# Expert weights w1 and w3 in chunks of 1024 columns in place of 512, in a two-layer encoder with eight experts

## The reference: what is computed

```python
def swiglu(x, w1, w3, w2):
    return (jax.nn.silu(x @ w1) * (x @ w3)) @ w2

def moe_swiglu(h, router_w, w1, w3, w2):
    logits = (xf @ router_w).astype(jnp.float32)
    top_val, top_idx = lax.top_k(logits, TOP_K)
    gates = jax.nn.softmax(top_val, axis=-1)
    ...
    y = lax.map(expert_block, (buf_tok.reshape(n_blocks, EXPERT_BLOCK), block_exp))
    y = y.reshape(P, D) * buf_g[:, None].astype(y.dtype)
```

## Time and profile before

| | us |
|---|---|
| time, three runs | 1866.17, 1866.32, 1866.81 |
| median | 1866.32 |
| span of the profiled execution, first to last instruction | 1863.3 |
| PE busy with matmuls | 1699.1 (91%) |
| DVE busy | 1319.9 (71%) |
| ACT busy | 1015.6 (55%) |
| POOL busy | 58.0 (3%) |
| share of DMA queue 1, 473 MB | 70.2% of 16 engines' span |

### The profile page before, as it was taken

The page is one execution under the profiler, slowest core; times in us unless marked ns, Lnnn a source line. Parts: engine busy times, 40 slices in busy tenths (PEclk is TensorE's granted clock), DMA queues, the critical chain, the costliest instruction groups (busy, mean ns, idle before and its releaser), DMA issues.

```text
span 1863.3 us, 23242 instructions
## 1 busy us (share of the span) xinstructions
PE 1699.1 (91%) x8214; PEld 1387.5 (74%) x8215; DVE 1319.9 (71%) x1525; ACT 1015.6 (55%) x1259; POOL 58.0 (3%) x52
## 2 busy tenths in 40 slices
PE   2996799999998999799999997997997997997998
PEld 2854699997677787588887785786786786786786
DVE  6597388885333799355554996896896896896897
ACT  1215344442322787344443875885775785775775
POOL 0000000000000100000000100100100100100100
PEclk7997899999998999899999998998998998999999
DMA  9972357867622499355553997897897898798790
GB/s 344 359 271 91 99 215 282 318 247 272 225 91 90 180 365 369 112 193 186 181 181 137 327 373 251 318 372 260 298 373 280 288 372 291 271 367 312 262 370 25
DMA packets 206838, 475.89 MB, mean 255 GB/s; under 512 B 6429, under 2 KB 8618, under 8 KB 206650
## 3 DMA queue, kind: packets, MB, share of 16 engines
q1 hardware_dynamic: 206442, 473.45, 70.2%
q10 hardware_dynamic: 208, 0.07, 0.0%
HBM read 472.46 MB, written 1.05 MB: 254 GB/s over the span
## 4 chain that ended last, share of the span: by engine, by line
PE 86%; DVE 6%; issue 5%; ACT 2%; DMA 1%; SPq 0%; DVEq 0%; ACTq 0%
PE bank L894 18%; PE bank L896 18%; PE bank L895 18%; PE bank L555 9%; PE bank L836 3%; PE bank L659 2%; PE bank L660 2%; PE bank L661 2%; PE bank L548 2%; PE bank L846 2%; PE bank L903 1%; DVE ada_acc L1257 1%; DVE w_lo L1562 1%; PE bank L679 1%; PE bank L677 1%
## 5 line engine op out<-in xcount | busy, mean ns | idle before, releaser
L1562 DVE TENSOR_TENSOR w_lo<-ring,w_hi 128x1024 fp32r<-128x1024 f32 x672 | 830.1, 1245 | 271.1 <-ACT w_hi L1156 199.7
L1156 ACT ACTIVATE w_hi<-ring 128x1024 fp32r<-128x1024 f32 x672 | 713.2, 1061 | 302.1 <-PE bank L896 288.8
L894 PE MATMUL bank<-w_hi,hg_hi 128*128 128x512 f32 x1008 | 398.9, 396 | 4.7 <-DVE w_lo L1562 4.3
L896 PE MATMUL bank<-w_hi,hg_lo 128*128 128x512 f32 x1008 | 394.8, 392 | 0.0
L895 PE MATMUL bank<-w_lo,hg_hi 128*128 128x512 f32 x1008 | 394.3, 391 | 0.0
L894 PEld LDWEIGHTS bank<-w_hi,hg_hi 128*128 128x128 f32 x1008 | 189.0, 188 | 69.0 <-issue 9.7
L896 PEld LDWEIGHTS bank<-w_hi,hg_lo 128*128 128x128 f32 x1008 | 189.3, 188 | 41.5
L895 PEld LDWEIGHTS bank<-w_lo,hg_hi 128*128 128x128 f32 x1008 | 189.5, 188 | 30.4
L894 PE MATMUL bank<-w_hi,hid_hi 128*128 128x512 f32 x504 | 202.2, 401 | 0.1
L896 PE MATMUL bank<-w_hi,hid_lo 128*128 128x512 f32 x504 | 197.7, 392 | 0.0
L895 PE MATMUL bank<-w_lo,hid_hi 128*128 128x512 f32 x504 | 197.1, 391 | 0.0
(11 more groups left out here) (260 smaller groups left out, 1837.5 us busy)
## 6 DMA issues: line engine op xcount, KB each, us to landing
ring<-in_moe_w SPq DMA_DIRECT2D x168, 2048.0 KB, 8.2
ring<-in_ada_w SPq DMA_DIRECT2D x24, 2048.0 KB, 11.5
ring<-in_ffn_w SPq DMA_DIRECT2D x15, 2048.0 KB, 12.7
ring<-in_da_w_in SPq DMA_DIRECT2D x6, 2048.0 KB, 19.8
ring<-in_gla_w_in SPq DMA_DIRECT2D x6, 2048.0 KB, 11.3
ring<-in_da_w_out SPq DMA_DIRECT2D x2, 2048.0 KB, 11.1
ring<-in_gla_w_out SPq DMA_DIRECT2D x2, 2048.0 KB, 8.6
ring<-in_ffn_w SPq DMA_DIRECT2D x3, 1024.0 KB, 5.9
```

Source lines behind the costliest of these rows:

```text
L894: mm(out[:, :], xhi, whi[:, cs], start=first, stop=False)
L896: last = mm(out[:, :], xlo, whi[:, cs], start=False, stop=end)
L1156: A(w_hi[:, q % PIECES, :], raw_piece(q), ACT.Copy).then_inc(hi_done, 1)
L1562: v.tensor_tensor(w_lo[:, q % PIECES, :], raw_piece(q), w_hi[:, q % PIECES, :].bitcast(F32), ALU.subtract).then_inc(lo_done, 1)
```

## The change

Chunks of w1 and w3 have 1024 columns, the last one 512 (`ECW`), so an expert has four chunks in place of seven. A slot of a wide chunk is one half of the rows (four tiles of 128) with 1024 columns, so its rows are 4 KB as those of w2; a wide chunk takes two slots of w1, then two of w3, then the two of w2 of the chunk before. The number of slots, pieces, matmuls and bytes stays.

With one block of tokens, pieces are used in the order in which they lie. Each of the two halves of a w1 piece goes to a bank of its own (0 and 1), and of a w3 piece too (6 and 7). Silu, product, `hid_hi` and `hid_lo` come in pairs, on four occasions and not seven; a pair has the work of two of the old ones. The transposes, eight of them together, go to banks 4 and 5, and w3 of the next chunk waits for the product (`s_ea`) and no more for `hid_lo`. The product is written over silu and no more to `ada_acc`.

With two blocks, all eight banks are taken, and the halves of 512 columns are worked through as before (`halves_of_expert`): both w1 slots and both w3 slots of a wide chunk are read for the first 512 columns and again for the second.

SP waits for `slot_left`, which PE raises at the end of the first matmul of a slot's last piece, in place of `lo_done`. With two blocks a slot is only counted when all slots before it in the order have been left too (`hfreed`).

At an expert's start ACT and DVE split one piece, handle the gathered tokens, and then split two more. The four scattered banks are copied before pieces 2, 3, 4 and 5. The wait for `s_gl` on PE stands ahead of the branch.

```diff
+ECW = [1024, 1024, 1024, 512]
+ECH = len(ECW)
+EHALF = EF // FW
...
     for c in range(ECH):
-        order += [("w1", c), ("w3", c)]
+        order += [(what, c, part) for what in ("w1", "w3") for part in range(parts_of(c))]
         if c:
-            order += [("w2", c - 1)]
-    return order + [("w2", ECH - 1)]
+            order += [("w2", c - 1, part) for part in range(parts_of(c - 1))]
+    return order + [("w2", ECH - 1, part) for part in range(parts_of(ECH - 1))]
+
+def halves_of_expert(eorder):
+    slot_of = {key: i for i, key in enumerate(eorder)}
+    pieces = []
+    for s in range(EHALF):
+        c, h = divmod(s, 2)
+        for what in ("w1", "w3"):
+            if parts_of(c) == 2:
+                pieces += [(what, s, slot_of[what, c, part], kp, h, 4 * part + 2 * kp)
+                           for part in range(2) for kp in range(2)]
+            else:
+                pieces += [(what, s, slot_of[what, c, 0], p, None, 2 * p) for p in range(PPC)]
+        if s:
+            c, h = divmod(s - 1, 2)
+            pieces += [("w2", s - 1, slot_of["w2", c, h], p, None, p) for p in range(PPC)]
...
+    left_at = {}
+    for q, piece in enumerate(hpieces):
+        left_at[piece[2]] = q
+    hfreed, latest = {}, -1
+    for i in range(PER):
+        latest = max(latest, left_at[i])
+        hfreed[latest] = hfreed.get(latest, 0) + 1
...
-                    sp.wait_ge(lo_done, (e + back) * EQ + FQ + (j + 1) * PPC)
+                    sp.wait_ge(slot_left, (e + back) * PER + j + 1)
...
+            def expert_block(e):
...
+                            k, o = (4 * part + p, j) if parts_of(c) == 2 else (2 * p + j, 0)
+                            xhi, xlo = hg_hi[:, k, 0:P], hg_lo[:, k, 0:P]
+                            out = psum[(0 if what == "w1" else 6) + o]
...
+                        begun = mm(out[:, :], xhi, whi[:, cs], start=first, stop=False)
+                        if j == 0 and p == PPC - 1:
+                            begun.then_inc(slot_left, 1)
...
+            def expert_two_blocks(e):
...
+                            if b == 0 and j == 0 and q in hfreed:
+                                begun.then_inc(slot_left, hfreed[q])
...
-                    if q in (2, 5, 8, 11):
-                        copy_scattered(e, (q - 2) // 3)
+                    if q in (2, 3, 4, 5):
+                        copy_scattered(e, q - 2)
...
+                        for b in range(parts_of(c)):
+                            last = A(silu_e[:, b, :], psum[b][:, :], ACT.Silu)
...
+                        for b in range(parts_of(c)):
+                            last = v.tensor_tensor(silu_e[:, b, :], silu_e[:, b, :], psum[6 + b][:, :], ALU.mult)
```

More of the change, by code:

```diff
@@ L1176, in expert @@
-                    if what == "w3" and p == 0:
+                    what, c, part = eorder[i]
+                    if what == "w3" and q == PPC * first_slot["w3", c]:
                         act.wait_ge(w_free, e * EQ + FQ + PIECES + q)
                         if c:
-                            act.wait_ge(s_ea, e * ECH + c)
-                        for b in range(nb):
+                            act.wait_ge(s_et, e * EHALF + c)
+                        for b in range(parts_of(c)):
+                            last = A(silu_e[:, b, :], psum[b][:, :], ACT.Silu)
+                        last.then_inc(s_esl, EHALF - ECH + 1 if c == ECH - 1 else 1)
@@ new lines, in expert_block, with expert_two_blocks, split_up_to @@
+                    if q - 1 in turn_at:
+                        turn = turn_at[q - 1]
+                        act.wait_ge(s_et, e * EHALF + turn + 1)
+                        for b in range(parts_of(turn)):
+                            last = A(hid_1[0][:, turn % 2, b * 512:(b + 1) * 512], psum[4 + b][:, :], ACT.Copy)
+                        last.then_inc(s_hdh, EHALF - ECH + 1 if turn == ECH - 1 else 1)
+            def expert_two_blocks(e):
+                done = [0]
+                seen = set()
+                def split_up_to(q_end):
+                    while done[0] <= min(q_end, EQ - 1):
+                        q = done[0]
+                        if hpieces[q][2] not in seen:
+                            seen.add(hpieces[q][2])
+                            wait_landed(act, PRE + hpieces[q][2], e)
+                        act.wait_ge(w_free, e * EQ + FQ + q + 1)
+                        A(split_half(w_hi, q), raw_half_piece(q), ACT.Copy).then_inc(hi_done, 1)
+                        done[0] += 1
+                split_up_to(0)
+                gathered(e, 2 * P)
+                split_up_to(AHEAD)
+                gates_out(e, 2)
+                for q, (what, s, i, p, h, k0) in enumerate(hpieces):
+                    if q in (2, 3, 4, 5):
+                        copy_scattered(e, q - 2)
+                    split_up_to(q + AHEAD)
+                    if what == "w3" and q == hfirst["w3", s]:
+                        act.wait_ge(w_free, e * EQ + FQ + PIECES + q)
+                        if s:
+                            act.wait_ge(s_et, e * EHALF + s)
+                        for b in range(2):
@@ L1194, in _ @@
                 nb = act.value_load(nbk[0:1, bass.ds(e, 1)], min_val=1, max_val=2)
-                for n in (1, 2):
-                    with act.If(nb == n):
-                        expert(e, n)
+                with act.If(nb == 1):
+                    expert_block(e)
+                with act.If(nb == 2):
+                    expert_two_blocks(e)
         @block.vector
```

273 lines of the change are left out of this document (189 added, 84 removed).

## The result

The changed kernel takes 1906.27 us, the median of four runs (1906.04 to 1907.79), against 1866.24 of the kernel before (1865.00 to 1866.81): a ratio of 1.0215 (95% interval 1.0200 to 1.0229; the later ratios have theirs in brackets). The forecast was 1910 us, slower. The profiled execution has a span of 1904.2 us; against 1863.3 before that is +40.9.

A forecast was written before the change was run, and what follows sets the result against it. PE was taken to bound the experts, with DVE close behind in one-block ones. Terms of 31 (one-block experts), 8 (ring), 3 and 2 (slot release) made +44 on 1863.3: 1907 span, 1910 us forecast; 8-in-10 range 1878 to 1928.

The forecast's parts named there:

- PE bounds the experts, with 0.22 us of spare time a piece: Within experts: PE is the bound; anything over 0.22 us done in one go on ACT or DVE stops it.
- Copies close together: +2.4 us an expert: One-block experts: four copies with POOL's adds one piece apart cost 3.6 us against 1.2 before, +2.4 an expert.
- Pairs: +2.1: One-block experts: paired work on ACT and DVE costs 1.6 and 1.2 us, less 0.7 of small waits, +2.1 an expert.
- DVE and POOL exclude each other: At the copies: POOL's add and DVE's `w_lo` do not run together, so a piece takes 2.39 us.
- the rival of shared bandwidth: At the copies: DVE and POOL each run slower; four adds cost 2.2 us, +1.0 an expert; no chance given.
- The ring in the two-block expert: +8: Two-block expert: w2 in slot 14 waits for twice-read slot 7; PE stands 7.8 us, +8 with some low clock.
- Slots released by PE: +3 and +2: Experts' ends: later release delays the gather, +3 us out of the two-block expert, +2 over six one-block ends.
- a gather 3 us sooner: Ends of experts: the forecast is wrong if the gathers come 3 us sooner or more.
- code that is fetched behind the weights: Before the gathers: inferred, not shown, reading of PE's idle time, 11.19 us at a one-block end, 4.59 after two-block.
- Absorbed bursts: One-block experts: pairs and adds cost PE no more than now; ring and ends remain, 1879 us; chance 0.10.
- The faster one (code arrives sooner): Seven ends of experts: idle time shrinks from 11.2 to 4.6 us, -46 in all, giving 1861 us; chance 0.06.
- the ends' terms: Ends of experts: the costs put on PE's later slot release, +3 us out of the two-block expert, +2 at one-block ends.

The follow-up runs named there:

- Experiment 1: The changed kernel with the four copies of scattered banks put back before pieces 2, 5, 8 and 11 in the one-block body: 1895.66 us, ratio 1.0162.
- Experiment 2: The changed kernel with the two w2 slots loaded between w1 and w3 of chunks 1 and 2, not behind w3: 1896.98 us, ratio 1.0168.
- Experiment 8: The kernel before, with SP waiting for the first matmul of a slot's last piece, not DVE's last split: 1866.93 us, ratio 1.0003.
- experiments 1 and 3: Beside Experiment 1: the changed kernel with paired silus, products and `hid_lo` separated by one split, wide chunks' transposes one piece later: 1900.80 us, ratio 1.0188.
- experiment 4: The kernel before, with the last two of the next expert's first seven loads held until three of its pieces are split: 1845.93 us, ratio 0.9891.

## Why the prediction was right

Nearly every step held, and one had the wrong sign.

- **PE bounds the experts, with 0.22 us of spare time a piece.** Held: what went beyond it, at the adds and at the pairs, stopped PE. The one-block experts cost +30.4 us, forecast +31.
- **Copies close together: +2.4 us an expert.** The cycle was worked out as 2.39 us a piece; it is 2.24, since the add ends 1.16 us after the `w_lo` before it and not 1.31. The loss at the adds is 3.5 us (3.6 forecast), but it had been 1.7 before and not 1.2, because two of the adds that seemed hidden, the second and the fourth, cost PE 0.2 to 0.3 each. So the term was +1.8 for what was put at +2.4. Experiment 1 gives 1.5 an expert.
- **Pairs: +2.1.** Silu pairs cost 0.51 us each (0.54 forecast), DVE pairs 0.52 (0.4). Together 3.1, where 2.8 had been put; the small waits and transposes fell by 0.7 (5.1 to 4.4 in the table), as taken off. The two errors, in adds (0.6 too much) and in pairs (0.3 too little), went opposite ways. That the sum hit so well is partly this, and so luck.
- **DVE and POOL exclude each other.** Held, and the rival of shared bandwidth falls. Wherever the two meet, in all the traces, an add ends 1.13 to 1.18 us after the `w_lo` it began beside, and a `w_lo` ends 1.08 to 1.15 us after the add it began beside. The product, which reads one buffer and a bank, ran beside an add without making it longer. With both the rule of the Trainium skill (SBUF — State Buffer, "SBUF: two separate sides") agrees.
- **The ring in the two-block expert: +8.** The place, the releaser and the length were right: 8.36 us, where 7.8 had been worked out. The low clock behind the stop was underrated: "a little" was 2 us. Experiment 2 removes all of it. The formula of the Trainium skill (DMA: Bandwidth & Descriptors, on the fixed and the variable component), which that page fits to transfers issued by GpSimd, gives an estimated stop of 6.8 us by the same sum. The trace, with 8.36, is further from that.
- **Slots released by PE: +3 and +2.** This step failed. I let the gather follow the last load's landing. It follows PE's jump instead: the later release cleared the DMA queues while PE fetched its code, and the gather came 3.3 us sooner (1.7 us after the last matmul, for 5.0), not 3 later. The prediction had named a gather 3 us sooner as a sign of being wrong; it came at this end, not at the others. At the one-block ends the cost is +0.1 to +0.6 each, 2.1 in all, as forecast. Experiment 8 has the release alone, and there the two cancel (-3.4 and +3.6). Had the reading "code that is fetched behind the weights" been followed to its end, it would have given this sign: the jump began at 1001.44 with the load of 999.79 in flight, and a load issued 3 us later leaves its first half free.
- **Rivals.** Absorbed bursts fall by the experts' +30.4 and by experiments 1 and 3. The faster one (code arrives sooner) was wrong for this change: at the one-block ends the jumps still have the weights' traffic beside them, and the gathers come no sooner. Its mechanism is real and worth 20 us where it is brought about on purpose, in experiment 4. Its price was wrong: without the ends' terms the sum is 39 and not 41, and only six ends had over 11 us to lose, 42 us in all, so it would have given 1863 us.

With the right sign of that end (-3.3 for +3) the sum would have been +38, and +40.9 was measured. Of the rest 2.4 us are in the two-block expert (10.4 for 8, mostly the clock) and 1.3 between gathers and first matmuls, for which nothing had been put; the one-block experts took 0.6 less. That 1910 lies within 4 us of 1906 is thus partly luck: 6.3 us of wrong sign against these smaller ones.

## What to carry to other kernels

Work out the spare time of the engine behind the bottleneck for one unit, here 0.22 us in 1.37: what is done "in pairs" beyond it became a stop, whatever the average load says, and the same four adds cost 3.5 us together and 1.7 three pieces apart. In a ring, look for a slot that is read twice: its successor landed late by a whole load. And keep bulk loads quiet over a loop's jump; holding two of seven back, and putting POOL's adds where DVE is idle, took 1.5 to 1.7% off a kernel whose bound, PE, was 91% busy.

## What the runs showed of the hardware beyond that

- **A jump of PE's sequencer took longer while weights were being loaded.** Out of the two-block expert 3.5 to 3.6 us with 6 to 24 GB/s of traffic in the 4 us around its start, 6.9 with 347. At the one-block ends the two jumps of experiment 4's table were longer by 1.1 and 1.4 us. Why the second stays near 5 us without traffic is open: ACT and DVE fetch code in the same time (queue 14 has packets too), but no run took that away.
- **After the 8 us without a matmul** in the two-block expert the granted clock is 0.50, and about ten matmuls start 0.2 us later each before it is back at its upper level.
- **Longer rows.** The 4 KB rows cut the packets of the weights' queue from 206,442 to 157,290, and the median load of the experts lands after 7.8 us, before after 8.2. No gain in any kernel here could be put down to it: apart from the two-block expert's stop, no expert's PE waits for a load.
